# The order of three routing tiles, and of the scatters and row gathers behind them, in a one-core streaming encoder layer

## What is computed

```
s1, i1 = lax.top_k(s[:, :, 0], PEER_TOPK)
s2, i2 = lax.top_k(s[:, :, 1], PEER_TOPK)
...
best, sel = lax.top_k(cand, PEER_TOPK)
eidx = jnp.take_along_axis(cidx, sel, axis=-1)
g = jax.nn.softmax(best, axis=-1)
u = jnp.take(u_tab, eidx, axis=0)
a = jax.nn.gelu(jnp.einsum('thkd,td->thk', u, xb).astype(jnp.float32))
vv = jnp.take(v_tab, eidx, axis=0)
return jnp.einsum('thk,thkd->td', (g * a).astype(xb.dtype), vv)
```

## Time and profile before

| | us |
|---|---|
| median of 3 runs | 2699.81 |
| lowest, highest | 2692.62, 2700.85 |
| the profiled execution: its own time | 2690.44 |
| the profiled execution: span | 2688.9 |
| PE busy | 2445.1 (91%) |
| DVE busy | 1922.5 (71%) |
| POOL busy | 1171.5 (44%) |
| ACT busy | 932.1 (35%) |

### The profile page before, as it was taken

One profiled execution on the slowest core, in us unless ns is written; L12 is line 12 of the kernel. 1 busy time (PEld: TensorE's weight loads), 2 busy tenths in 40 slices (PEclk: granted clock), 3 DMA queues, 4 the chain that ended last, 5 costly groups with the idle time before them and its releaser, 6 DMA issues.

```text
span 2688.9 us, 38865 instructions
## 1 busy us (share of the span) xinstructions
PE 2445.1 (91%) x13838; PEld 2182.7 (81%) x13838; DVE 1922.5 (71%) x2105; ACT 932.1 (35%) x1018; POOL 1171.5 (44%) x684
## 2 busy tenths in 40 slices
PE   5988989889899999999989988989999999898999
PEld 4867768768699899999988888989877777777777
DVE  4554544543446999999877776777679888888888
ACT  3353443532323333333323222323433333423323
POOL 1020100120000001057888888883576676767662
PEclk9999989989999999999999998999999999999999
DMA  5443444458255557778889998998899999999997
GB/s 192 130 159 117 136 135 129 149 215 313 80 123 105 159 166 221 214 209 214 218 225 253 238 248 237 245 234 226 291 393 392 411 403 397 387 399 382 392 396 307
DMA packets 280168, 661.43 MB, mean 246 GB/s; under 512 B 73144, under 2 KB 123128, under 8 KB 237911
## 3 DMA queue, kind: packets, MB, share of 16 engines
q1 hardware_dynamic: 154832, 334.57, 38.4%
q0 software_dynamic: 82064, 249.26, 27.2%
q10 hardware_dynamic: 43191, 76.58, 10.0%
HBM read 613.65 MB, written 46.02 MB: 245 GB/s over the span
## 4 chain that ended last, share of the span: by engine, by line
PE 37%; POOL 22%; DMA 17%; DVE 13%; issue 7%; ACT 2%; DVEq 1%; ACTq 1%; SPq 0%; POOLq 0%
POOL g_dense L494 15%; PE banks L1293 11%; PE banks L1294 11%; PE banks L1295 11%; DVE h L1245 4%; DMA raw<-in_v_tab 4%; POOL a_values L536 4%; DMA v_raw<-in_v_tab 3%; DMA v_row<-in_v_tab,route_place 2%; POOL u_row L488 2%; DMA raw<-in_u_tab 2%; DMA k_cache<-in_cache_k 2%; DMA a_tile<-a_dense 1%; DVE u_turned L1122 1%; DVEq L842 1%
## 5 line engine op out<-in xcount | busy, mean ns | idle before, releaser
L1293 PE MATMUL banks<-xT_hi,ring_hi 128*128 128x320 f32 (+1 forms) x2304 | 735.1, 319 | 80.3 <-DVE ring_lo L1126 72.9
L1294 PE MATMUL banks<-xT_lo,ring_hi 128*128 128x320 f32 (+1 forms) x2304 | 729.5, 317 | 0.0
L1295 PE MATMUL banks<-xT_hi,ring_lo 128*128 128x320 f32 (+1 forms) x2304 | 729.0, 316 | 0.0
L494 POOL DMA_INDIRECT g_dense<-route,route_place x256 | 498.9, 1949 | 128.5 <-issue 77.1
L1293 PEld LDWEIGHTS banks<-xT_hi,ring_hi 128*128 128x128 f32 x2304 | 442.7, 192 | 91.0 <-issue 79.4
L1294 PEld LDWEIGHTS banks<-xT_lo,ring_hi 128*128 128x128 f32 x2304 | 443.1, 192 | 0.0
L1295 PEld LDWEIGHTS banks<-xT_hi,ring_lo 128*128 128x128 f32 x2304 | 442.4, 192 | 0.0
L527 POOL DMA_INDIRECT v_row<-in_v_tab,route_place x128 | 288.3, 2252 | 185.7 <-DVE h L1245 162.6
L863 DVE TENSOR_TENSOR ring_lo<-raw,ring_hi 128x2048 fp32r<-128x2048 f32 x72 | 164.6, 2291 | 264.9 <-ACT ring_hi L574 264.6
L1126 DVE TENSOR_TENSOR ring_lo<-u_turned,ring_hi 128x2048 fp32r<-128x2048 f32 x128 | 290.3, 2268 | 58.5 <-ACT ring_hi L780 57.3
L1122 DVE STREAM_TRANSPOSE u_turned<-raw 128x2048 f32<-128x2048 f32 x128 | 295.6, 2309 | 50.3 <-DMA raw<-in_u_tab 42.3
(11 more groups left out here) (219 smaller groups left out, 3820.8 us busy)
## 6 DMA issues: line engine op xcount, KB each, us to landing
raw<-in_u_tab SPq DMA_DIRECT2D x512, 128.0 KB
raw<-in_u_tab ACTq DMA_DIRECT2D x512, 128.0 KB
v_raw<-in_v_tab SPq DMA_DIRECT2D x64, 1024.0 KB, 11.3
raw<-in_v_tab SPq DMA_DIRECT2D x64, 1024.0 KB, 11.5
raw<-in_w_in SPq DMA_DIRECT2D x160, 256.0 KB
a_dense<-gelu_out SPq DMA_DIRECT2D x128, 160.0 KB
raw<-in_w_out SPq DMA_DIRECT2D x64, 256.0 KB
g_dense<-zeros POOLq DMA_DIRECT2D x16, 1024.0 KB, 25.5
```

What stands on the lines that cost most here:

```text
L494: pool.indirect_dma_start(out=places, out_offset=bass.IndirectOffsetOnAxis(ap=routeU[:, t, 2, j:j + 1], axis=0), in_=route[:, t, 0, j:j + ...
L1293: MM(out, h1, h2, start=first, stop=False)
L1294: MM(out, h1, l2, start=False, stop=False)
L1295: return MM(out, l1, h2, start=False, stop=last)
```

## The change

The prompt tile 0 is routed first (steps 5 to 17), the sample tile 2 second (steps 18 to 30, with no dots), and prompt tile 1 last, a part in every second step from 31 to 55, with a dot in the steps between (13 dots until step 56). The other 51 dots go over the 66 steps from 57 on. POOL starts with scatters, in 64 groups of 4 instead of 32 of 8, and takes the first ten groups (40 scatters) before any gather; then it waits for tile 2's routing, copies the indices, and gathers 4 rows; after that a group of 4 scatters is laid to 1.25 steps, with gathers up to `dots_after(step + 1) + NUB`. Nothing is added or removed: 256 scatters, 64 gathers, 64 dots, 39 routing parts. All else in the file is the same, its lines below L494 shifted by two.

```
-TILE_ORDER = (2, 0, 1)
-ALONE = N_SWEEPS + N_PARTS
-MIXED = ALONE + 3 * N_PARTS - 1
+TILE_ORDER = (0, 2, 1)
+FIRST, SECOND = N_SWEEPS + N_PARTS, N_SWEEPS + 2 * N_PARTS
+MIXED = SECOND + 2 * N_PARTS
...
-    if m >= ALONE:
-        i = N_PARTS + (m - ALONE) // 3 * 2 + (m - ALONE) % 3 if (m - ALONE) % 3 < 2 else -1
+    if m >= SECOND:
+        i = 2 * N_PARTS + (m - SECOND) // 2 if (m - SECOND) % 2 == 0 else -1
...
     if m < MIXED:
-        return max(m + 1 - ALONE, 0) // 3
-    done = (MIXED - ALONE) // 3
+        return max(m + 1 - SECOND, 0) // 2
+    done = (MIXED - SECOND) // 2
     return min(DOTS, done + (m + 1 - MIXED) * (DOTS - done) // 66)
...
-            while gathered < dots_after(MIXED - 2 * N_PARTS) + NUB:
-                gather_dot(gathered)
-                gathered += 1
-            for n in range(TD // P * PH * 2):
-                t, h, half = n // (2 * PH), n // 2 % PH, n % 2
-                if n % (2 * PH) == 0:
-                    pool.wait_ge(rt_ready, t + 2)
-                if half == 0 and n:
-                    pool.wait_ge(g_scat, 16 * (n // 2 * TOPK))
-                for k in range(half * TOPK // 2, (half + 1) * TOPK // 2):
+            for n in range(TD // P * PH * 4):
+                t, h, part = n // (4 * PH), n // 4 % PH, n % 4
+                if n == 0:
+                    pool.wait_ge(rt_ready, 1)
+                elif n == 4 * PH:
+                    pool.wait_ge(rt_ready, 3)
+                if part == 0 and n:
+                    pool.wait_ge(g_scat, 16 * (n // 4 * TOPK))
+                for k in range(part * 4, part * 4 + 4):
                     scatter(t, h * TOPK + k)
-                while gathered < min(DOTS, dots_after(38 + (n + 1) * 5 // 2) + NUB):
+                step = FIRST + 1 + (n + 1) * 5 // 4
+                if step < SECOND:
+                    continue
+                if not gathered:
+                    pool.wait_ge(rt_ready, 2)
+                    pool.dma_start(uidx[0:GT, :], routeU[own, NT - 1, 1, 0:DOTS]).then_inc(uidx_in, 16)
+                    pool.dma_start(uidx[own, :], routeU[own, NT - 1, 1, DOTS:SLOTS]).then_inc(uidx_in, 16)
+                    pool.wait_ge(uidx_in, 32)
+                while gathered < min(DOTS, dots_after(step + 1) + NUB):
                     gather_dot(gathered)
                     gathered += 1
```

More of the change, by code:

```diff
@@ L478, in _ @@
             pool.dma_start(xrow[0:GT, :], xrow[own, :]).then_inc(xrow_in, 16)
[L479 to L482, removed]
             def gather_dot(i):
```

## The result

| | before | changed |
|---|---|---|
| median us | 2697.41 | 2711.41 |
| lowest, highest | 2685.96, 2708.99 | 2700.22, 2718.63 |
| runs | 15 | 15 |

The ratio to before is 1.0053, 95% interval 1.0038 to 1.0068: slower by 14 us, where 18 us faster and a median of 2682 were forecast, above the range's end of 2702. A second set of runs gave 1.0041 (1.0012 to 1.0071). The profiled execution of the changed kernel took 2718.6 us, the longest of its runs (that of before, 2690.4, is one of the shorter), so the 28 us between the two profiles are about twice the difference of the medians; a second profile of the changed kernel (span 2714.6 us) stands with the experiments.

What follows compares the result with a forecast made beforehand. The prediction took POOL's issue as the bound: 1140.6 + 486 + 75 = 1701.8, then + 64.5 + 122.4 = 1888.7 us for the last gelu, against 1906.7. Hence 2699.8 - 18.0 = 2681.8 us, range 2660 to 2702.

Steps and rivals of the forecast that it cites:

- What bounds the kernel: U stage, 1323 to 1840 us: POOL's issue is the bound, without a free moment; the stage loses 110.5 us.
- Start, first forty scatters, fourth gather: POOL's beginning: first scatter at about 1024.2 us, forty scatters taking 90 us until 1114, fourth gather at about 1140.6.
- To add nothing for DVE: Steps 18 to 30, full of routing: the forty scatters beside them do not lengthen DVE's instructions, so 0 us added.
- Rival B: Steps 18 to 30: scatters hold DVE up, routing of tile 2 ends later; 2722 to 2760 us, chance 0.05.
- POOL is without pause from there, 486 + 75 us: POOL from the fourth gather at 1140.6 us: 216 scatters 486 us, 45 gathers 75 us, last scatter ends at 1701.8.
- whether POOL would wait for a dot: POOL between the fourth gather and the last scatter: no wait, as each group takes longer than DVE's 8.8 us.
- The scatter's price: POOL, for each of 216 scatters: 2.25 us with its gap, bounds 2.15 to 2.35, or 21.6 us either way.
- The price of a gather: POOL, for each of 45 gathers up to row 47: 1.67 us with its gap, 75 us in all.
- From row 48 to the end of the stage, 64.5 + 122.4 us: U stage's end: 64.5 us as before plus 17 steps of 7.2 us, last gelu at 1888.7 us, 18.0 sooner.
- rival A: U stage: transfers become the bound, steps behind the last scatter cost 7.6 to 7.8 us; about 2693 us, chance 0.18.
- Waits of DVE for rows: In the changed profile: DVE's waits for gathered rows fewer in total and in shorter pieces; before, 68.9 us.
- The chances: For the whole kernel: faster by over 0.3% 0.75, within that 0.17, slower 0.08.

Runs made afterwards that it cites:

- spread version: The changed kernel with 4 scatters laid to 1.5625 steps instead of 1.25, all else as changed; ratio to before 0.9755, median 2635.94 us.
- half scatters: The changed kernel with only every second scatter, 128 of 256, leaving out half of the prompt tiles' weights; ratio to before 0.9732.
- groups of eight: The changed kernel with its scatters in 32 groups of 8 again, 8 to 2.5 steps; ratio to before 1.0007, median 2700.93 us.
- paced rows: The changed kernel with groups of eight, rows from row 50 on gathered one by one, each three steps before its dot; ratio to before 1.0008.

## Why the prediction was wrong

**What bounds the kernel: right.** POOL's issue, between the third routing and step 120. The spread version and the half scatters both show it, with waits of DVE for rows that vanish with POOL's load.

**Start, first forty scatters, fourth gather: right**, within about 5 us each. To add nothing for DVE beside the forty scatters was right too: from step 18 to step 31 the gelus lose 3.7 us over 7.04 a block, and 3.8 from step 5 to step 18, where there are no scatters. What the Trainium skill's page "SBUF — State Buffer", section "Who interferes with whom", says of the pair being held by whichever starts first does not show in DVE's instructions here; this trace disagrees, with dots of 2276 to 2294 ns. The page also ties that contention, for a DVE instruction with two inputs, to a GpSimd instruction that reads SBUF, a condition that the prediction left out. It is POOL's instructions that get longer here, as the last section shows. Rival B did not happen, though the result is on its side.

**"POOL is without pause from there, 486 + 75 us": the step that failed, 561 for 594 us** (590 in the second profile). The last scatter ends at 1730.3, not 1701.8. POOL did pause, by two waits that the sum put at nothing:

| from the fourth gather to the end of the last scatter, us | forecast | changed | second profile |
|---|---|---|---|
| 216 scatters with their gaps | 486 | 493.1 | 495.8 |
| 45 gathers with their gaps | 75 | 79.5 | 71.6 |
| waits for landed scatters | 0 | 14.5 | 15.4 |
| waits for dots | 0 | 7.1 | 7.1 |

Over half of the miss are the two waits. The question whether POOL would wait for a dot was asked and answered with no; it waited three times, at 1154, 1171 and 1200 us. The wait for sixteen landed scatters was 1.2 us in the kernel before, hidden behind gathers, and the prediction did not ask what groups of four would uncover. The scatter's price came out at 2.28 and 2.30 us, inside its bounds but above the 2.25. The price of a gather, 1.67 us, lies between the two profiles' 1.77 and 1.59. With groups of eight the end agrees, 1701.6 against 1701.8, partly by luck: that stretch took 566 us and not 561, and began 5 us sooner.

**"From row 48 to the end of the stage, 64.5 + 122.4 us": too small, by 14 us in the change, 19 with groups of eight.** In the change the 17 steps took 7.97 us each where 7.2 was taken, 135.5 us for 122.4, which is nearly all of the 14. With groups of eight the last gelu follows the last scatter's end by 205.8 us, not 186.9; the 17 steps took 7.7 us each (119.7 us at 7.04 and 11.6 lost), which is about 9 of the 19: late raw blocks, as in rival A (DVE waits 18.4 us for them from 1735 to 1860 us there, 20.6 in the change). The DMA share is 0.96 at 274 GB/s from 1700 to 1800 us in that kernel. This is read from the waits; the one run aimed at these steps, the paced rows, did not shorten them. The other 10 lie in how far DVE stands behind at that moment, which the prediction set equal in both kernels: the gelu of step 103 comes 24.2 us after the last scatter's end, where before, the gelu of step 120, whose row is the one behind the last scatter there, comes 14.5 us after it. So rival A priced the steps of this kernel rightly (7.6 to 7.8) and those of the change a little low; it takes the 10 us as well, and a V stage 4 us longer, to cancel the gain, and the small groups come on top.

**Waits of DVE for rows** were forecast to be fewer in total and in shorter pieces. They grew, 103.5 us for 68.9 in the stage, the longest 10.5 us for 9.3.

**The chances.** The only way to a slower kernel that the prediction saw was DVE held up by scatters. It saw that the order of POOL's queue changes in its pieces, but gave that change no price and no bounds; with the landing wait in the sum the slower side would have got more than 0.08.

**The larger miss** is in the question. The prediction found that the order "still lays four scatters to 1.25 steps, more than POOL can do", and stopped there. That one number was worth 3% of the kernel, nearly six times what the change cost.

What stays open: why a scatter itself takes 2004 and 2036 ns and not 1947 in the busy stretch with groups of four, and why the V stages of all the later kernels are 784 to 791 us long where that of before is 782.

## What to carry to other kernels

When an engine that issues is the bound because a fixed order asks it for more per step than it can do, an earlier start helps only if the rate is lowered with it; work out (instructions per step) x (price) against the step and stretch the work until it fits. Where instructions of one kind stand in pieces, ask which wait a piece hides before cutting it up. Before a difference of a few microseconds between two profiles is called the price of an order, profile one of the kernels a second time. When a wait of the bound goes, look at what share the next resource already has.

## What was not expected of the hardware

**The clock falls behind a stall.** A stretch of the changed kernel in four windows (PE, PE's weight loads, DVE, ACT and POOL busy; PEclk; DMA share; GB/s):

```profile
1362.00:1366.00 4.00, 4.00 (x29) 4.00 (x28) 0.00 (x0) 2.17 (x2) 3.09 (x4) 1.00 0.81 159
1366.00:1370.00 4.00, 2.82 (x20) 2.56 (x18) 0.00 (x0) 0.44 (x1) 3.39 (x3) 1.00 0.85 270
1370.00:1374.00 4.00, 0.00 (x0) 0.00 (x0) 2.66 (x3) 0.00 (x0) 3.39 (x3) 0.87 0.50 54
1374.00:1378.00 4.00, 0.00 (x0) 0.00 (x0) 4.00 (x3) 0.20 (x1) 3.39 (x3) 0.50 0.98 399
```

DVE waits 10.51 us for a gathered row here, PE runs out of work at about 1369, and the granted clock goes from 2.4 to 1.2 GHz at 1372.9, where it stays for 10.2 us. PE starts again at 1378.17, and its matmuls are then 0.27 us apart, where they were 0.15 apart before the stall:

```profile
1354.14 0.31 PE L1295 MATMUL banks<-xT_hi,ring_hi 128*128 128x320 f32 x1
1354.29 0.31 PE L1296 MATMUL banks<-xT_lo,ring_hi 128*128 128x320 f32 x1
...
1378.17 0.63 PE L1295 MATMUL banks<-xT_hi,ring_hi 128*128 128x320 f32 x1 [9.35 <-DVE ring_lo L1128]
...
1379.13 0.47 PE L1295 MATMUL banks<-xT_hi,ring_hi 128*128 128x320 f32 x1
1379.40 0.47 PE L1296 MATMUL banks<-xT_lo,ring_hi 128*128 128x320 f32 x1
```

Between the first and the last gelu the changed kernel has 78 us at 1.2 GHz (75 in its second profile), the one before 65, the one with groups of eight 55 (72 in its paced twin), the spread version 14 (by the records of the granted clock in each trace). So a DVE stall costs PE more than its own length, and part of what the spread version gains is clock: PEclk is 0.92 and 0.93 in the changed kernel's two long windows above, 0.98 and 1.00 in its.

**What an indirect DMA costs POOL hangs on what DVE does beside it, not on its place in a piece.** Three gathers in a row behind the last scatter of the groups-of-eight kernel, and what DVE does meanwhile:

```profile
1701.93 0.99 POOL L483 DMA_INDIRECT u_row<-in_u_tab,u_index  x1 [0.30 <-issue]
1703.23 2.97 POOL L483 DMA_INDIRECT u_row<-in_u_tab,u_index  x1 [0.30 <-issue]
1706.50 0.94 POOL L483 DMA_INDIRECT u_row<-in_u_tab,u_index  x1 [0.30 <-issue]
...
1698.45 2.31 DVE L1124 STREAM_TRANSPOSE u_turned<-raw 128x2048 f32<-128x2048 f32 x1
1703.06 2.29 DVE L1128 TENSOR_TENSOR ring_lo<-u_turned,ring_hi 128x2048 fp32r<-128x2048 f32 x1 [2.30 <-ACT ring_hi L782]
```

The first is cheap and the second dear: it lies beside the subtraction (L1128), which like the dot reads two inputs. In the changed kernel, from 1323 us on, the 21 gathers with no subtraction or dot beside them took 0.94 to 1.00 us, and the 29 with one 1.67 us on average; the 38 scatters with none took 1.55 to 1.60 us, the 109 with one 2.16. The turn (L1124), with one input, costs them nothing. With half of the scatters 61 of the 64 gathers are released by the end of a dot, most of them alone between scatters. None of the 48 from 1323 us on has a subtraction or a dot beside it, and a gather costs 1.0 us:

```profile
L483 POOL DMA_INDIRECT u_row<-in_u_tab,u_index x64 | 65.5, 1024 | 341.8 <-DVE a_dots L1199 339.9 <-DMA u_index<-route_place 1.4 <-issue 0.6
```

DVE's own instructions take no more time for it, as the dots of 2276 to 2294 ns above show.
